# Spatial gating unit with channels in partitions: mixing product turned over, gating half computed turned, mixing weights loaded turned

## What is computed

```python
def gmlp_branch(z, ln_g, ln_b, w_s, b_s):
    z = jax.nn.gelu(z, approximate=False)
    u, v = jnp.split(z, 2, axis=-1)
    v = layer_norm(v, ln_g, ln_b).reshape(B, S // C, C, G, CH)
    w = w_s * jnp.tril(jnp.ones((C, C), dtype=w_s.dtype))
    vs = jnp.einsum('gts,bnsgc->bntgc', w, v) + b_s.T[None, None, :, :, None]
    return u * vs.reshape(B, S, GMLP_WIDTH)
```

## Time and profile before

| | |
|---|---|
| median of 3 runs | 2056.66 us |
| the profiled execution | 2056.99 us |
| its span, first to last instruction | 2055.2 us |
| mean granted TensorE clock | 0.998 |
| PE busy | 2040.3 us, 10357 matmuls |
| PEld (weight loads) busy | 1718.7 us |
| DVE busy | 1390.4 us |
| ACT busy | 1018.4 us |
| POOL busy | 76.0 us |
| HBM read | 374.53 MB |

### The profile page before, as it was taken

One profiled execution on the slowest core, in us unless ns is written; L12 is line 12 of the kernel. 1 busy time (PEld: TensorE's weight loads), 2 busy tenths in 40 slices (PEclk: granted clock), 3 DMA queues, 4 the chain that ended last, 5 costly groups with the idle time before them and its releaser, 6 DMA issues.

```text
span 2055.2 us, 25142 instructions
## 1 busy us (share of the span) xinstructions
PE 2040.3 (99%) x10357; PEld 1718.7 (84%) x10357; DVE 1390.4 (68%) x1638; ACT 1018.4 (50%) x1290; POOL 76.0 (4%) x119
## 2 busy tenths in 40 slices
PE   9999999999999999999999999999999999999998
PEld 7888888888888888888888888888888888888887
DVE  6545686775757666787575667657767667577676
ACT  6444486454435345675444365644534466544331
POOL 1000000000010001000100000000100000000000
PEclk9999999999999999999999999999999999999999
DMA  8655454475656555544666474554755645455552
GB/s 311 209 188 184 164 170 144 137 222 186 193 189 223 187 177 193 171 141 147 204 198 190 159 243 144 177 164 167 239 190 186 204 154 185 156 191 186 194 193 83
DMA packets 223729, 377.20 MB, mean 184 GB/s; under 512 B 6544, under 2 KB 109072, under 8 KB 223616
## 3 DMA queue, kind: packets, MB, share of 16 engines
q1 hardware_dynamic: 219504, 362.31, 53.6%
q0 software_dynamic: 3824, 12.97, 2.1%
q10 hardware_dynamic: 288, 0.33, 0.1%
HBM read 374.53 MB, written 1.05 MB: 183 GB/s over the span
## 4 chain that ended last, share of the span: by engine, by line
PE 95%; DVE 2%; ACT 1%; DMA 1%; issue 0%; POOL 0%; DVEq 0%; ACTq 0%
PE pb L1585 63%; PE pb L1596 16%; PE pb L1599 9%; PE pb L1608 2%; DMA raw<-in_ffn_w_up_dram 1%; PE pb L1654 1%; DVE wl L2054 0%; PE pb L1732 0%; DVE lS L2241 0%; ACT wh L1826 0%; DVE st L2247 0%; DVE st L2246 0%; DMA raw<-in_ffn_w_gate_dram 0%; PE pb L1719 0%; PE pb L1796 0%
## 5 line engine op out<-in xcount | busy, mean ns | idle before, releaser
L1826 ACT ACTIVATE wh<-raw 128x2048 fp32r<-128x2048 f32 (+4 forms) x351 | 658.6, 1877 | 640.2 <-PE pb L1585 284.5
L2054 DVE TENSOR_TENSOR wl<-raw,wh 128x2048 fp32r<-128x2048 f32 (+4 forms) x351 | 783.1, 2236 | 167.6 <-ACT wh L1826 166.9
L1585 PE MATMUL pb<-wh,x 128*128 128x512 f32 (+1 forms) x2224 | 676.3, 386 | 0.0
L1585 PEld LDWEIGHTS pb<-wh,x 128*128 128x128 f32 x2224 | 415.7, 188 | 80.9
L1585 PE MATMUL pb<-wl,x 128*128 128x512 f32 (+2 forms) x1112 | 438.8, 395 | 0.1
L1596 PE MATMUL pb<-x,wh 128*128 128x512 f32 x1504 | 379.6, 394 | 0.0
L1596 PEld LDWEIGHTS pb<-x,wh 128*128 128x128 f32 x1504 | 271.5, 189 | 49.5
L1585 PE MATMUL pb<-wl,mh 128*128 128x512 f32 (+1 forms) x740 | 255.8, 391 | 0.9 <-issue 0.9
L1585 PE MATMUL pb<-wh,ml 128*128 128x512 f32 (+1 forms) x740 | 253.7, 388 | 0.0
L1585 PE MATMUL pb<-wh,mh 128*128 128x512 f32 (+1 forms) x740 | 253.5, 388 | 0.0
L1585 PEld LDWEIGHTS pb<-wl,x 128*128 128x128 f32 x1112 | 208.9, 188 | 45.0 <-issue 3.7
(11 more groups left out here) (361 smaller groups left out, 1581.0 us busy)
## 6 DMA issues: line engine op xcount, KB each, us to landing
raw<-in_w_in_dram SPq DMA_DIRECT2D x100, 1024.0 KB, 5.2
raw<-in_w_ff_dram SPq DMA_DIRECT2D x64, 1024.0 KB, 5.2
raw<-in_ffn_w_down_dram SPq DMA_DIRECT2D x44, 1024.0 KB, 4.9
raw<-in_ffn_w_up_dram SPq DMA_DIRECT2D x43, 1024.0 KB, 5.4
raw<-in_ffn_w_gate_dram SPq DMA_DIRECT2D x42, 1024.0 KB, 5.3
raw<-in_w_branch_dram SPq DMA_DIRECT2D x24, 1024.0 KB, 5.0
raw<-in_w_out_dram SPq DMA_DIRECT2D x16, 1024.0 KB, 5.0
raw<-in_w_in_dram SPq DMA_DIRECT2D x4, 832.0 KB, 4.5
```

Source lines behind the costliest of these rows:

```text
L1585: ins = e.matmul(pb[b][:, 0:c1 - c0], x[:, s, cols], w[:, n, c0:c1], start=(it["first"] and n == 0 and q == 0), stop=(it["stop"] and n == ...
L1826: e.activation(hi, raw, ACT.Copy).then_inc(m.high_done, 1)
L2054: e.tensor_tensor(lo, raw, hi.bitcast(F32), ALU.subtract).then_inc(m.low_done, 1)
```

## The change

The gating unit is computed with channels in partitions throughout. The mixing weights come turned from the host and go straight into `wsT`, so `wsturn` is gone, and `wsmask` works in place. `zmix` exchanges its operands: `zv` is stationary, `wsT` moves, and the result comes out turned. The half u is computed by wide visits into `zuT` (two units of 8 x 256 instead of two of 4 x 512), whose halves DVE adds (`wadd`) and over which ACT then goes with Gelu in SBUF (`wgelu`, one for each unit). `zgate` adds a bias that was loaded into all partitions (`bs`) and multiplies by `zuT`. The two `turn` groups of `zu` are gone; one `zsplit` makes `yph` and `ypl` from `zuT`. `gmlp(t)` now enters its lane when half t of v is done.

```diff
@@ memory
-        self.ws = A("ws", o_be, [P, 4, P])
+        self.bs = A("bs", o_be, [P, 4, P])
-        self.zu = A("zu", o_xn, [P, 2, 512])
+        self.zuT = A("zuT", o_xn, [P, 4, S])
@@ mixer2
         def wst():
             for _ in range(8):
                 yield
-            use = self.side()
-            v = self.pe("wsturn", use=use, l=l)
-            self.add("wsmask", use=use, p=v["p"], l=l)
-            self.ws = ("evac", use)
-            yield
-            yield
+            self.add("wsmask", l=l)
             self.add("wgusplit", l=l)
-        def gelu(b, dst, toks):
-            def epi(t, p, uses):
-                self.add("gelu", dst=dst, t=t, p=p, use=uses[0])
-                toks[t] = ("evac", uses[0])
-                if b == 1:
-                    self.lanes[3].append(gmlp(t))
+        def gelu_v(t, p, uses):
+            self.add("gelu", dst="zv", t=t, p=p, use=uses[0])
+            zv[t] = ("evac", uses[0])
+            self.lanes[3].append(gmlp(t))
+
+        def gelu_u(q):
+            def epi(i, p, use):
+                self.add("wadd", dst=("zuT", q), i=i, p=p, use=use, free=None)
+                if i:
+                    n = self.next("zu")
+                    self.later.append(lambda: self.add("wgelu", q=q, use=use))
+                    zu.append(("zu_done", n + 1))
             return epi
@@ gmlp(t), behind znorm
             yield
             yield
+            while len(zu) < 2:
+                yield
+            yield
             use = self.side()
-            v = self.pe("zmix", t=t, use=use, need=[("zv_done", n + 1), self.ws])
-            self.add("zgate", t=t, use=use, p=v["p"], l=l, need=[zu[t]])
-            yield
-            yield
-            gm_done.append(self.turn("Y", 0, t, ("zu", t), 4, [("evac", use)]))
+            v = self.pe("zmix", t=t, use=use, need=[("zv_done", n + 1), ("ws_masked", l + 1)])
+            self.add("zgate", t=t, use=use, p=v["p"], l=l, need=zu[1:])
+            gm_done.append(use)
+            if t:
+                yield
+                self.add("zsplit", n=l, need=self.last_of(gm_done))
...
-        self.group(self.cols(W, l, 2576, 0, gelu(0, "zv", zv)) + self.cols(W, l, 2064, 1, gelu(1, "zu", zu)))
+        self.group(self.cols(W, l, 2576, 0, gelu_v))
+        for q in range(2):
+            self.wide_group((W, (l,), 0, 8, 2064 + 256 * q, 256), self.pair(q), gelu_u(q))
@@ pool_program, loads2
-            e.dma_start(m.ws[:, :, :], m.A["gmlp_w_s_2"][l].rearrange("g t s -> t g s")).then_inc(m.ws_landed, 16)
+            e.dma_start(m.wsT[:, :, :], m.A["gmlp_w_s_2"][l]).then_inc(m.ws_landed, 16)
+            e.dma_start(m.bs[:, :, :], m.A["bs"][l].partition_broadcast(P)).then_inc(m.bs_landed, 16)
@@ pe_program
-        elif k == "wsturn":
...
-            for g in range(4):
-                ins = e.transpose(bank[:, g * P:g * P + P], m.ws[:, g, :], ident[:, :])
-            ins.then_inc(m.pe_done, 1)
         elif k == "zmix":
...
-                ins = e.matmul(bank[:, c], m.wsT[:, g, :], m.zv[:, t, c], start=True, stop=True)
+                ins = e.matmul(bank[:, c], m.zv[:, t, c], m.wsT[:, g, :], start=True, stop=True)
@@ act_program
+        elif k == "wgelu":
+            q = it["q"]
+            a.emptied(use)
+            e.activation(m.pair_of(("zuT", q)), m.pair_of(("zuT", q)), ACT.Gelu).then_inc(m.zu_done, 1)
+        elif k == "zsplit":
+            a.all_ready(it["need"])
+            e.activation(m.yph[:, :, :], m.zuT[:, :, :], ACT.Copy).then_inc(m.z_high, 1)
@@ dve_program
         elif k == "wsmask":
-            v.pe(p)
             v.wait_ge(m.tril_landed, 16 * (l + 1))
-            e.tensor_tensor(m.wsT[:, :, :], bank[:, :].rearrange("p (g t) -> p g t", g=4),
-                            m.tril[:, :].unsqueeze(1).broadcast_to([P, 4, P]), ALU.mult).then_inc(m.evac[use[0]], 1)
+            v.wait_ge(m.ws_landed, 16 * (l + 1))
+            e.tensor_tensor(m.wsT[:, :, :], m.wsT[:, :, :], m.tril[:, :].unsqueeze(1).broadcast_to([P, 4, P]),
+                            ALU.mult).then_inc(m.ws_masked, 1)
         elif k == "zgate":
...
-            for g in range(4):
-                u = m.zu[:, t, g * P:g * P + P]
-                ins = e.scalar_tensor_tensor(u, bank[:, g * P:g * P + P], m.gp[:, 5 + g:6 + g], u, ALU.add, ALU.mult)
-            ins.then_inc(m.evac[use[0]], 1)
+            mixed, u = bank[:, :].rearrange("p (g n) -> p g n", n=P), m.zuT[:, :, t * P:t * P + P]
+            v.step(e.tensor_tensor(mixed, mixed, m.bs[:, :, :], ALU.add))
+            v.own_steps()
+            e.tensor_tensor(u, mixed, u, ALU.mult).then_inc(m.evac[use[0]], 1)
+        elif k == "zsplit":
+            v.wait_ge(m.z_high, n + 1)
+            e.tensor_tensor(m.ypl[:, :, :], m.zuT[:, :, :], m.yph[:, :, :].bitcast(F32), ALU.subtract).then_inc(m.z_low, 1)
@@ layouts (host)
+    a["gmlp_w_s_2"] = a["gmlp_w_s_2"].transpose(0, 3, 1, 2)
+    a["bs"] = g["gmlp_b_s_2"]
```

More of the change, by code:

```diff
@@ L107, in __init__ @@
         self.ws_landed, self.lng_landed, self.gp_landed = s("ws_landed"), s("lng_landed"), s("gp_landed")
+        self.bs_landed, self.ws_masked, self.zu_done = s("bs_landed"), s("ws_masked"), s("zu_done")
+        self.z_high, self.z_low = s("z_high"), s("z_low")
         self.lr_high, self.wgu_high, self.wgu_low = s("lr_high"), s("wgu_high"), s("wgu_low")
@@ L127, in __init__ @@
                       "weights_ready": self.weights_ready, "y_low": self.y_low, "x_low": self.x_low,
-                      "mo_low": self.mo_low, "kr_saved": self.kr_saved}
+                      "mo_low": self.mo_low, "kr_saved": self.kr_saved, "ws_masked": self.ws_masked,
+                      "zu_done": self.zu_done, "z_low": self.z_low}
     def sem(self, name):
@@ L273, in sbuf @@
                       "Y": (self.yph, self.ypl)}
-        self.rows = {"pin": self.pin, "dv": self.dv, "v": self.v, "mv": self.mv, "gv": self.gv, "zu": self.zu, "gg": self.gg,
+        self.rows = {"pin": self.pin, "dv": self.dv, "v": self.v, "mv": self.mv, "gv": self.gv, "gg": self.gg,
                      "zv": self.zv, "cn": self.cn}
         self.cols = {"dqT": self.dqT, "dkT": self.dkT, "gqT": self.gqT, "gkT": self.gkT,
-                     "pT": self.pT}
+                     "pT": self.pT, "zuT": self.zuT}
     def unit(self, j):
@@ L1211, in mixer2 @@
         self.clear("Y", range(4))
-        gm_done, zv, zu = [], {}, {}
+        gm_done, zv, zu = [], {}, []
         first = []
@@ L1239, in gmlp @@
             yield
+            while len(zu) < 2:
+                yield
+            yield
             use = self.side()
-            v = self.pe("zmix", t=t, use=use, need=[("zv_done", n + 1), self.ws])
-            self.add("zgate", t=t, use=use, p=v["p"], l=l, need=[zu[t]])
-            yield
-            yield
-            gm_done.append(self.turn("Y", 0, t, ("zu", t), 4, [("evac", use)]))
+            v = self.pe("zmix", t=t, use=use, need=[("zv_done", n + 1), ("ws_masked", l + 1)])
[4 more added lines that the diff above has]
+                self.add("zsplit", n=l, need=self.last_of(gm_done))
+                for s in range(4):
+                    for u in range(2):
+                        self.ready["Y", s, u] = ("z_low", l + 1)
         self.lanes[3].append(wst())
@@ L1272, in decay @@
                 v = self.pe("decay", i=i, use=use, need=lr, l=l)
-                self.add("logsig", i=i, use=use, p=v["p"], n=2 * l + i, l=l, war=gm_done[1])
+                self.add("logsig", i=i, use=use, p=v["p"], n=2 * l + i, l=l, war=self.last_of(gm_done))
                 yield
@@ L1732, in pe_program @@
             e.matmul(bank[:, 128:384], Q[0:w, P:S], key, start=True, stop=True).then_inc(m.pe_done, 1)
-        elif k == "wsturn":
-            bank = pb[use[0]]
-            pe.wait_ge(m.ws_landed, 16 * (l + 1))
-            pe.wait_ge(m.evac[use[0]], use[1])
-            for g in range(4):
-                ins = e.transpose(bank[:, g * P:g * P + P], m.ws[:, g, :], ident[:, :])
-            ins.then_inc(m.pe_done, 1)
         elif k == "zmix":
@@ L1966, in act_program @@
             e.activation(m.row(it["dst"], t), bank[:, :], ACT.Gelu).then_inc(m.evac[use[0]], 1)
+        elif k == "wgelu":
[5 more added lines that the diff above has]
+            e.activation(m.yph[:, :, :], m.zuT[:, :, :], ACT.Copy).then_inc(m.z_high, 1)
         elif k == "logsig":
             a.pe(p)
-            a.pe(it["war"])
+            a.all_ready(it["war"])
             a.wait_ge(m.gp_landed, 16 * (l + 1))
@@ L2321, in dve_program @@
             v.all_ready(it["need"])
-            v.wait_ge(m.gp_landed, 16 * (l + 1))
-            for g in range(4):
-                u = m.zu[:, t, g * P:g * P + P]
-                ins = e.scalar_tensor_tensor(u, bank[:, g * P:g * P + P], m.gp[:, 5 + g:6 + g], u, ALU.add, ALU.mult)
-            ins.then_inc(m.evac[use[0]], 1)
+            v.wait_ge(m.bs_landed, 16 * (l + 1))
```

(2 more changed lines are left out.)

## The result

| | before | changed |
|---|---|---|
| median | 2056.62 us (16 runs) | 2060.69 us (16 runs) |
| profiled execution, span | 2056.99, 2055.2 us | 2060.51, 2058.3 us |

The ratio is 1.0021, with a 95% interval of 1.0014 to 1.0028: 4.1 us slower, and 2060.6 was predicted. Why is not known. The runs of the changed kernel lie in two groups: nine from 2060.0 to 2060.7 us, six from 2061.6 to 2062.2, and one at 2065.0.

The account below looks back on a forecast made before the run. PE, busy 99% of the span, was taken as the bound. Per layer -1.7 us work and +2.8 wait, +2.2 for two layers, plus 1.7 clock on 2056.99: 2060.9, or 2060.6 against the median; 8-in-10 range 2056.5 to 2063.5.

Parts of the forecast that it names:

- Work taken out: Three transpose groups and the `zmix` wait leave PE, 1.8 us a layer; net of dearer wide visits, 1.7 us less.
- `zmix` no longer waits: PE's wait in `zmix` for `zv` goes because `znorm` stands far ahead; taken as 0.4 us a layer.
- The new wait: PE stands still before the third `pscore`, waiting for ACT's `lQ`: about 2.8 us in each layer, bounds none to 3.5.
- Clock, one fall for two holes: PE's clock drops behind one of the two layers' holes, adding 1.7 us; 24%.
- The start row: At the trace start PE stood still 1.9 us, then lost 1.7 us to the lower clock; taken against the 3 us rule.
- The rule of 3 us: Skill's rule: only idle gaps over some 3 us matter, so both holes pass at full clock: 2058.9 us; 24%.
- No hole: Rival: the third `lQ` is in time and only the PE work goes: -3.4 us, 2053.3 us; 13%.
- Second wait: Rival: PE also waits at the fourth head's `pturn`, some 1.5 us a layer: 2063.6 us; 12%.
- Dearer table switches: Rival: changing ACT's table set costs more than its load, each hole 1.3 us longer: 2063.2 us; 2%.

Follow-up runs that it names:

- run 5: Changed kernel with first `znorm` two yields later and one Gelu over all of `zuT`, placed behind the fourth head's exponentials: 2052.79 us, ratio to before 0.9981.
- run 1: Changed kernel with only the first `znorm` four yields later, behind the third head's softmax: 2055.11 us, ratio to the kernel before 0.9993.
- run 3: Changed kernel with one Gelu over all of `zuT` in place of one for each unit: 2054.55 us, ratio to the kernel before 0.9988.
- run 6: Changed kernel with one Gelu over `zuT` and two more ACT copies ahead of the third head's `lQ` copy: 2056.76 us, ratio to before 1.0000.
- run 7: Changed kernel with one Gelu over `zuT` and three more ACT copies ahead of the third head's `lQ` copy: 2058.13 us, ratio to before 1.0010.
- run 8: Changed kernel, otherwise as it was, with two more ACT copies ahead of the third head's `lQ` copy: 2064.14 us, ratio to the kernel before 1.0037.
- run 4: Changed kernel with first `znorm` four yields later and one Gelu over all of `zuT`: 2054.88 us, ratio to the kernel before 0.9992.

## Why the prediction was right

- **Work taken out, -1.7 us a layer**: right in kind, 0.1 to 0.3 us a layer too small. The measure above gives 1.8 (447.5 - 445.7), but its end lies inside layer 1. A wider one runs from a wait of PE that both kernels have (852.53 before, 852.08 in run 5) to the first product with `gv` in layer 0 and from there to the last in layer 1. Before, and below it run 5:

```profile
L1783 PE MATMUL pb<-gv,lG x16: 272/322/373, 1324.5 to 1784.7; 64*128 64x128 f32 x16
```

```profile
L1795 PE MATMUL pb<-gv,lG x16: 272/322/373, 1322.0 to 1780.2; 64*128 64x128 f32 x16
```

The first part takes 469.9 instead of 472.0 us, the second 458.2 instead of 460.2: 2.0 to 2.1 us a layer, together the 2056.92 - 2052.79 = 4.1 us of the medians. In run 1 the second part takes 459.2, which with its wait of 0.83 leaves 1.8. Only `wsturn`, 0.5, was measured by itself; which of the other items is larger than counted is open.
- **`zmix` no longer waits**: right, the row is gone.
- **The new wait, 2.8 us**: right in place, releaser, count and size (2.80 and, from 1681.74, 2.78). The run came to the stretch 0.23 us earlier than counted (last `pnorm` step at 1237.71 for 1237.94); with this added each step of the chain holds: `znorm` to its follower 1241.79 + 0.23 = 1242.02 (1242.04 counted), softmax 1245.42 (1245.44), third `lQ` ready 1252.08 (1252.07). That the causes are those two, `znorm` ahead of the second softmax and the table load with Gelu ahead of `lQ`, is shown by runs 1 and 3, which take away one each.
- **Clock, one fall for two holes, 1.7 us**: right for the profiled execution. The 1.7 was the size of every fall seen. The "one of two" was the middle of the bounds and had no reason behind it, so that it came out is luck; runs 6 to 8 show what the bounds hide. In the stretch, holes of 0.8 and 1.8 us had no fall in either layer, of 2.3 and 2.8 in one of two, of 3.8 in both. Of each size above 0.8 us these are only two holes, from one execution. The six runs some 1.4 us above the nine would fit a second fall by their size, but the record speaks rather against it: their mean clock is 0.998, as in seven of the nine, and run 8, whose profiled execution has a fall in both layers, has 0.997 in all five. What makes the two groups stays open.
- **The start row as a guide** was half right. It said that 1.9 us suffice; in the stretch 1.8 us did not, twice. And the fall at the start seems to cost nothing. In runs 1, 4 and 5, whose first wait was 1.2 to 1.4 us, the clock stayed at 1.00 in the window of the earlier trace rows, yet PE came no 1.7 us earlier to the second block (its wait near 852 us stands at 852.67, 852.29 and 852.08, and at 852.31 in run 3, which has the fall). That the fetches bound the start at either clock (DMA share 1.05 in the earlier trace rows) is the likely reason, not a tested one.
- **The rule of 3 us.** The Trainium skill ("TensorE: Matmul & The Clock Gate", section "Why this matters for your kernels") wants no idle gaps over some 3 us. Above it the rule held (run 8, both holes). Below it is not safe: 2.3 and 2.8 us cost a fall each in one of two layers, and 2.7 near the start in both executions that had such a hole (runs 6 and 7).
- **Rivals.** No hole: fell here, and is what run 5 makes of it. Second wait: fell in the changed kernel, where the last `pnorm` step of the fourth head ended at 1261.47 and its `pturn` came at 1265.13; in run 3, with the loads in the same place and a hole of only 0.83, it still ended 0.5 us ahead (1261.19, 1261.72). The wait of 0.83 us at this `pturn` in runs 1 and 4 has another cause than the rival's: the exponentials waited for DVE, where `znorm` now stood, and not for the loads. Dearer table switches: fell. Gelu starts 1.29 us after its load; taking load and Gelu away made `lQ` 1.97 us earlier, against 1.29 + 0.54 by start to start. What is left, 0.14 us, is the most that this change of set can have cost beyond its load; the Trainium skill ("ScalarE: Activation LUTs", section "What ACT_TABLE_LOAD costs") gives a drain of 1.38 us, which does not show here.
- **The number, 2060.6 for 2060.69**: closer than its terms. The work term was up to 0.6 us too small over both layers, and the 0.3 us outside the span, which no term had, make up for part of that; the profiled execution took 3.5 us more than before where 3.9 were forecast.

So the change is a gain of some 4 us in PE work that was turned into a loss by the order that came with it: 2 x 2.8 us of waiting and a fall of 1.7. With the order mended it is faster than the kernel before by 4.1 us, 0.2%.

## What to carry to other kernels

On a kernel with PE at 99%, count what a change takes out of PE, and then walk the in-order queues of the other engines from the moved step to the next thing PE wants from them, with start-to-start times; four transposes were worth 0.48 us, one layer norm ahead of the wrong softmax 2.8. A step that must stand somewhere on DVE goes where the head behind it has the most to spare, which a trace of the neighbouring order tells at once. A hole of PE may cost another 1.7 us of clock (here from 2.3 us on in the stretch), so shortening two of them from 2.8 to 0.8 us brought 6.1 us (2060.69 to 2054.55), 0.3 of it outside the span, and not 4.0.

## What was not expected

- Two holes of equal length (2.14 us in the brackets of run 7, 2.64 and 2.62 in the changed kernel) differ in whether the clock falls behind them. Between 1.8 us (none of two) and 3.8 (two of two) length alone does not decide. What does was not tested.
- A fall always had the same size, 1.7 us lost by the clock, whatever the hole.
- The fall in the first 12 us of the trace brought no delay that shows at 852 us.
- The time outside the span differs by 0.3 us between runs 1 and 4 (2.1 and 1.8 us), which differ only in the Gelu of `zuT`.
